# Six column sums of squares as two fp32r products each, with the sums split in place by ScalarE and GpSimd

## The chip, the cores and the metric

The kernel runs on one core of a Trainium2 chip. Times are device microseconds of one launch: the median of three runs was 1108.56 us, from 1108.11 to 1109.01. In the text TensorE is PE, VectorE DVE, ScalarE ACT, GpSimd POOL, and SyncE SP, as in the profile.

## The reference

One residual block on a sequence of 1024 tokens with 1024 features, in float32:

```python
h = rmsnorm(x, g_mix);  z = h @ w_in                      # 1792 columns: LRU input, LRU gate, q, k, v
lx = causal_depthwise_conv(z[..., :512]);  y_lru = rg_lru(lx, ...)
y_lru = rmsnorm(y_lru * gelu(z[..., 512:1024]), g_lru_out)
y_att = rmsnorm(chunk_window_attention(q, k, v, sinks), g_attn_out)
x = x + concatenate([y_lru, y_att]) @ w_out
h = rmsnorm(x, g_ffn);  x = x + square(relu(h @ w_ff1)) @ w_ff2
gate = sigmoid(rmsnorm(x, g_ple) @ w_ple_gate);  x = x + gate * (p @ w_ple_proj)
return rmsnorm(x, g_final)
```

with `rmsnorm(x, g) = x * rsqrt(mean(x * x, axis=-1) + 1e-6) * g`. There are six normalizations, and each needs the sum of squares over the features of every token.

## The kernel before

Activations lie transposed: features on the 128 partitions, tokens along a row. `xT` holds 8 feature tiles of 1024 tokens. Nearly every product is done in three fp32r passes (`passes`, L565 to L569): both operands are split into a high part (fp32r, a rounded copy by ACT) and a low part (the difference, by DVE or POOL), and PE does high by high, high by low and low by high. Halves of 512 tokens are worked one after the other; a PSUM bank holds 128 x 512.

A sum of squares comes about in four steps. ACT squares one feature tile into a ring of two (`square`, L906, or `final_square`). DVE or POOL adds it to a running total of 128 x 512 (`add_square`, L331, or `final_add`, L540), in the tiles `acc` and `acc2`; a square may be written once the one two before it was added (`sq_used`). PE then multiplies the total by a 128 x 128 tile of ones (`sum_rows`, L609), which adds over the partitions and leaves the result on all of them. This product is in plain float32, and the profile shows it as two matmul instructions. ACT takes the root (`root`, L915), DVE inverts it (`invert`, L1286).

There are twelve such sums, two for each of `SS_MIX`, `SS_LRU`, `SS_ATT`, `SS_FFN`, `SS_PLE`, and two of the three parts of `SS_FIN` (512, 256 and 256 tokens; the third part is summed at L874 to L878 and isn't among the twelve). For LRU, PLE and FIN it is POOL that adds the squares.

The order on each engine is the order of the code. Around the six sums of LRU, PLE and FIN it is this:

- LRU. PE runs `group(g)` for g = 0 to 27, each 24 matmuls (5.5 us). Behind group 22 comes the sum of the first half, behind group 23 that of the second, which also waits until ACT has taken the first root (`pe.wait_ge(rms_done, n)`); both use bank 5. Each is followed by a turn of part of v (`turn_v`). Group 24 needs the first half of piece 6 of the weights, split by POOL (`low(12)`, line L444), which stands on POOL right behind the squares' sums. ACT does the squares at g = 20 and 21, reads v at the end of g = 21, and takes the roots at g = 22 and 23.
- PLE. The first sum stands ahead of the gate's cells on PE, the second behind cells 0 to 3. Between the adds of the two, POOL splits four half pieces of the gate's weights.
- FIN. The gate is computed in 20 cells (`CELLS`), each an eight-step product; a cell is 512 tokens wide for q below 12 and 256 for q from 12 on. For each cell DVE scales (`gate_scale`), ACT takes the sigmoid, DVE multiplies and adds into `xT` (`gate_add`), ACT squares, POOL adds. The first sum of FIN stands behind cells 12 and 13 on PE (it covers cells 0 to 3 and 8 to 11, whose last add is q = 11), the second inside cell 17, behind its first step (last add q = 15). The third part is scaled and stored at the end.

Of the kernel before, what the change touches and what calls it, by code (L numbers as in the profile page):

```python
# [13 lines left out]
P = 128  # L14
# [66 lines left out]
RING_FREE = 2  # L81
PRODUCTS = 7
# [11 lines left out]
def build(nc, x, p, vectors, gates_w, w_in, w_out, w_ff1, w_ff2, w_ple_gate, w_ple_proj, alibi, out):  # L94
    ctx = ExitStack()
    with ctx:
# [33 lines left out]
        r_lru = at("r_lru", G + 12 * KB, [P, SEQ])  # L130

# [37 lines left out]
        acc2 = at("acc2", KV + 4 * (PAD + SEQ), [P, SEQ])  # L169

        at_byte = KV + 2 * 4 * (PAD + SEQ)
        small = {}
        for name, shape in (("r_mix", [P, SEQ]), ("ident", [P, P]), ("ones", [P, P]), ("vec", [P, NVEC]),
                            ("nsink", [P, 8]), ("eps", [P, 1]),
                            ("lam", [P, 6, LT]), ("nmax", [P, 2, 8]), ("smax", [P, 2, 8]),
                            ("esink", [P, 2, 8]), ("den", [P, 2, 8])):
            small[name] = at(name, at_byte, shape)
            at_byte += -(-4 * int(np.prod(shape[1:])) // 32) * 32
        r_mix, ident, ones, vec = (small[n] for n in ("r_mix", "ident", "ones", "vec"))
        relu = at("relu", KV + 2 * 4 * (PAD + SEQ), [P, 2, HALF])  # L180
        nsink, eps, lam = (small[n] for n in ("nsink", "eps", "lam"))
# [18 lines left out]

        consts, w_split, sq_used, p_ready, pool_chain = (
# [31 lines left out]
        def half(hf):  # L233
            return slice(hf * HALF, (hf + 1) * HALF)
# [11 lines left out]
        def right(i, h, t):  # L246

            return (h[:, 0:LT, half(1)], t[2], t[1], t[3], h[:, LT:KD, half(0)], h[:, LT:KD, half(1)], t[4])[i]

# [180 lines left out]
        def _(pool):  # L430
# [14 lines left out]

            def sums(n, ring, total):
                for i in range(SQ_TILES[n]):
                    add_square(pool, n, i, ring, total)
# [27 lines left out]
            for n in range(2, IN_PIECES):  # L476
                low(2 * n)
                low(2 * n + 1)
                if n - 2 < LT:
                    gate_input_low(n - 2)  # L480
                if n == 5:
                    sums(SS_LRU, sq, acc)
                    sums(SS_LRU + 1, sq, acc)
# [51 lines left out]
            low(2 * GATE_FIRST + 1)  # L535
            low(2 * (GATE_FIRST + 1))
            low(2 * (GATE_FIRST + 1) + 1)
            sums(SS_PLE + 1, sq2, acc2)

# [13 lines left out]
            for q in range(len(CELLS) - 2):  # L553
                final_add(q)

# [8 lines left out]
        def _(pe):  # L564
# [44 lines left out]
            def sum_rows(n, total, b):  # L609

                pe.wait_ge(sq_used, SQ_BY[n])
                if n >= 1:
                    pe.wait_ge(rms_done, n)
                tok, width = span(n)
                pe.matmul(bank[b][:, 0:width], ones[:, :], total[:, tok], start=True, stop=True  # L615
                          ).then_inc(ss_done, 1)
# [266 lines left out]
        def _(act):  # L883
# [26 lines left out]

            def unit_square(u):
                act.wait_ge(o_read, u + 1)
                square(SQ_BY[SS_ATT - 1] + u, sq, qT[:, 2 * u:2 * u + 2, :, :].rearrange("p c j q -> p (c j q)"))
# [9 lines left out]
            act.activation(lam[:, 2, :], ones[:, 0:LT], ACT.Square)  # L923
            act.wait_ge(first_w_in, 16)
# [49 lines left out]
            for g in range(IN_GROUPS):  # L974
# [16 lines left out]
                if g in (20, 21):  # L991
                    hf = g - 20
                    act.wait_ge(state_done, LT)
                    for j in range(LT):
                        act.wait_ge(y_done, j + 1)
                        square(SQ_BY[SS_LRU + hf] - 4 + j, sq, yl(j)[:, half(hf)])
                if g in (22, 23):
                    root(SS_LRU + g - 22, 5, r_lru, LRU)
# [199 lines left out]
            gate_high(GATE_FIRST)  # L1198
            keep(0)
# [28 lines left out]
            for q in range(len(CELLS)):  # L1228
                if q in (14, 17):
                    root(SS_FIN + (q == 17), 4, r_fin, D)  # L1230
                sigmoid(q)
                if q == 3:
                    root(SS_PLE + 1, 4, r_mix, D)
# [622 lines left out]
```

## Time and profile before

| | us |
| --- | --- |
| median of 3 runs | 1108.56 |
| the profiled execution, its own time | 1109.54 |
| its span | 1107.8 |
| PE busy | 1073.4 (97%) |
| DVE busy | 726.7 (66%) |
| ACT busy | 419.5 (38%) |
| POOL busy | 472.1 (43%) |

The span is the time from the first to the last instruction that the profile shows. Busy times are sums over the whole span; an engine with a low share can still be the one that is waited for in a stretch. The end of a matmul is modelled, so overlapping matmuls are read by their starts: from one start to the next is the time that one really takes of the engine.

### The profile page before, as it was taken

The numbers are of one execution on the slowest core, as the hardware profiler recorded it, in microseconds if no ns is written. First come the engines' busy times: TensorE is split into PE (matmuls) and PEld (weight loads), VectorE is DVE, ScalarE is ACT, GpSimd is POOL, SyncE is SP. The second block draws the span as 40 slices with busy tenths as digits, with TensorE's granted clock in tenths as the row PEclk, the third lists the DMA queues.
The fourth block names the chain that finished last, engine by engine and source line by source line (L and its number), as shares of the span: only waits on it lengthen the run. The fifth ranks groups of instructions, "written<-read, shape, count | busy, mean of one in ns | idle before, by whom it ended". The sixth has DMA issues, their size and how long they took to land.

```text
span 1107.8 us, 13619 instructions
## 1 busy us (share of the span) xinstructions
PE 1073.4 (97%) x4898; PEld 870.7 (79%) x4898; DVE 726.7 (66%) x921; ACT 419.5 (38%) x725; POOL 472.1 (43%) x304
## 2 busy tenths in 40 slices
PE   6899999899999999999999999999999999999995
PEld 5778888677876888888888888888888888888895
DVE  6997666889799836536536546546545545696557
ACT  7555664454456222222222222212312312565334
POOL 2744252333306256255255355355355355293221
PEclk9999999999999999999999999999999999999998
DMA  8211102111001211211211211211111101420004
GB/s 285 77 39 38 38 1 86 39 39 39 1 1 38 76 38 38 76 38 38 76 38 38 76 38 38 76 38 40 73 38 51 63 38 61 167 76 1 1 1 153
DMA packets 20162, 61.05 MB, mean 55 GB/s; under 512 B 2080, under 2 KB 4128, under 8 KB 20128
## 3 DMA queue, kind: packets, MB, share of 16 engines
q1 hardware_dynamic: 19584, 60.08, 15.2%
q10 hardware_dynamic: 544, 0.52, 0.1%
q8 instruction: 20, 0.33, 0.1%
q14 instruction: 14, 0.11, 0.0%
HBM read 56.40 MB, written 4.19 MB: 55 GB/s over the span
## 4 chain that ended last, share of the span: by engine, by line
PE 79%; DVE 11%; ACT 4%; issue 3%; POOL 2%; DMA 1%; SPq 0%; DVEq 0%; ACTq 0%
PE bank L567 26%; PE bank L568 25%; PE bank L569 25%; POOL w_lo L444 1%; DVE r_mix L1288 1%; DVE lane L1335 1%; DMA stage<-in_w_in 1%; DVE acc L343 1%; POOL gx_lo L473 1%; DVE r_ffn L1288 1%; PE bank L657 1%; PE bank L615 1%; DVE xT L1682 1%; DVE h_lo L1550 1%; DVE xT L1754 1%
## 5 line engine op out<-in xcount | busy, mean ns | idle before, releaser
L567 PE MATMUL bank<-h_hi,w_hi 128*128 128x512 f32 (+1 forms) x724 | 282.6, 390 | 13.7 <-DVE h_lo L1275 9.8
L568 PE MATMUL bank<-h_lo,w_hi 128*128 128x512 f32 (+1 forms) x724 | 276.7, 382 | 0.0
L569 PE MATMUL bank<-h_hi,w_lo 128*128 128x512 f32 (+1 forms) x724 | 276.4, 382 | 0.0
L1682 DVE TENSOR_TENSOR xT<-bank,xT 128x512 f32<-128x512 f32 x256 | 173.7, 688 | 114.0 <-PE bank L569 112.3
L567 PE MATMUL bank<-u_hi,w_hi 128*128 128x512 f32 x512 | 202.2, 395 | 2.4 <-DVE xT L1682 1.1
L569 PE MATMUL bank<-u_hi,w_lo 128*128 128x512 f32 x512 | 199.4, 389 | 0.0
L568 PE MATMUL bank<-u_lo,w_hi 128*128 128x512 f32 x512 | 199.4, 389 | 0.0
L567 PEld LDWEIGHTS bank<-h_hi,w_hi 128*128 128x128 f32 x724 | 137.0, 189 | 46.6 <-issue 16.1
L521 POOL TENSOR_TENSOR w_lo<-w_raw,w_hi 128x1024 fp32r<-128x1024 f32 x30 | 78.1, 2624 | 192.2 <-ACT w_hi L1152 192.2
L568 PEld LDWEIGHTS bank<-h_lo,w_hi 128*128 128x128 f32 x724 | 137.0, 189 | 27.0 <-issue 1.9
L569 PEld LDWEIGHTS bank<-h_hi,w_lo 128*128 128x128 f32 x724 | 137.0, 189 | 26.5
L567 PEld LDWEIGHTS bank<-u_hi,w_hi 128*128 128x128 f32 x512 | 96.0, 188 | 32.9 <-issue 7.6
L444 POOL TENSOR_TENSOR w_lo<-stage,w_hi 128x1024 fp32r<-128x1024 f32 x26 | 69.7, 2700 | 114.9 <-ACT w_hi L890 114.9
L569 PEld LDWEIGHTS bank<-u_hi,w_lo 128*128 128x128 f32 x512 | 96.1, 188 | 20.3
L568 PEld LDWEIGHTS bank<-u_lo,w_hi 128*128 128x128 f32 x512 | 96.1, 188 | 19.1
L1146 ACT ACTIVATE relu<-bank 128x512 f32<-128x512 f32 x15 | 9.0, 598 | 193.9 <-PE bank L569 193.9
L505 POOL TENSOR_TENSOR s_raw<-w_raw 128x512 f32<-128x512 f32 x15 | 20.4, 1362 | 144.6 <-DMA w_raw<-in_w_ff 144.6
L514 POOL TENSOR_TENSOR w_lo<-w_raw,w_hi 128x512 fp32r<-128x512 f32 x60 | 78.7, 1324 | 2.3 <-POOL s_raw L510 2.1
L514 POOL TENSOR_TENSOR s_lo<-s_raw,s_hi 128x512 fp32r<-128x512 f32 x45 | 58.9, 1324 | 0.0
L343 POOL TENSOR_TENSOR acc<-acc,sq 128x512 f32<-128x512 f32 x33 | 49.9, 1513 | 17.9 <-DVE acc L343 8.9
L1657 DVE TENSOR_TENSOR usq<-bank,relu 128x512 f32<-128x512 f32 x15 | 10.4, 691 | 68.9 <-PE bank L569 68.9
L1654 DVE TENSOR_TENSOR relu<-bank,relu 128x512 f32<-128x512 f32 x15 | 10.4, 690 | 66.5 <-PE bank L569 66.5
(208 smaller groups left out, 1694.6 us busy)
## 6 DMA issues: line engine op xcount, KB each, us to landing
w_raw<-in_w_ff SPq DMA_DIRECT2D x60, 512.0 KB, 3.7
stage<-in_w_in SPq DMA_DIRECT2D x13, 512.0 KB, 3.4
stage<-in_w_out SPq DMA_DIRECT2D x8, 512.0 KB, 3.5
stage<-in_w_ple_gate SPq DMA_DIRECT2D x8, 512.0 KB, 3.9
xT<-in_x SPq DMA_DIRECT2D x7, 512.0 KB, 9.7
stage<-in_w_ff SPq DMA_DIRECT2D x4, 512.0 KB, 3.2
out_x<-xT SPq DMA_DIRECT2D x4, 512.0 KB, 2.9
out_x<-xT SPq DMA_DIRECT2D x6, 256.0 KB, 2.9
```

The costliest lines, as they stand in the source:

```text
L343: eng.tensor_tensor(dst, dst, src, ALU.add).then_inc(sq_used, 1)
L444: pool.tensor_tensor(lo, stage[:, s % STAGES, :], hi, ALU.subtract).then_inc(w_split, 1)
L473: pool.tensor_tensor(gx_lo[:, half(hf)], yl(j)[:, half(hf)], gx_hi[:, half(hf)], ALU.subtract).then_inc(gx_low, 1)
L505: pool.tensor_tensor(s1, a21, a22, ALU.add).then_inc(s_made, 1)
L514: pool.tensor_tensor(left(i, w_lo, s_lo), left(i, w_raw, s_raw), left(i, w_hi, s_hi), ALU.subtract).then_inc(w1_split, 1)
L521: pool.tensor_tensor(w_lo[:, (FF_FIRST + 1) % 2, o], w_raw[:, (FF_FIRST + 1) % 2, o], w_hi[:, (FF_FIRST + 1) % 2, o], ALU.subtract).then_i ...
L567: pe.matmul(o, whi, hh, start=first, stop=False, skip_group_check=onto)
L568: pe.matmul(o, whi, hl, start=False, stop=False, skip_group_check=onto)
L569: return pe.matmul(o, wlo, hh, start=False, stop=last, skip_group_check=onto)
L615: pe.matmul(bank[b][:, 0:width], ones[:, :], total[:, tok], start=True, stop=True).then_inc(ss_done, 1)
L1288: link(dve.reciprocal(dst[:, span(n)[0]], dst[:, span(n)[0]]))
L1682: dve.tensor_tensor(dst, bank[4 + q % 4][:, :], dst, ALU.add).then_inc(y_added, 1)
```

## The change

Six of the twelve sums, those of LRU, PLE and FIN (`SPLIT_SUMS`), are done as two fp32r products. When all squares of such a sum are added, ACT copies the total into an fp32r tile (`total_head`), and POOL writes total minus that copy, as fp32r, over the total (`total_rest`). PE multiplies both by an fp32r tile of ones, which ACT makes once at the start, into the same bank. PE no longer waits for `sq_used` there but for `total_low`, which POOL raises. The high part lies where the root will be written (`r_lru`, `r_mix`, `r_fin`). The other six sums stay as they are.

```diff
--- before.py
+++ after.py
@@ -79,6 +79,7 @@
 SP_STORES, ACT_STORES = (slice(0, 2), slice(4, 6)), (slice(2, 4), slice(6, 8))
 POOL_OUT, DVE_OUT = (6, 7), range(6)
 RING_FREE = 2
+SPLIT_SUMS = (SS_LRU, SS_LRU + 1, SS_PLE, SS_PLE + 1, SS_FIN, SS_FIN + 1)
 PRODUCTS = 7
 
 
@@ -128,6 +129,8 @@
         lane = at("lane", T + 12 * KB, [P, LT + 1, SEQ])
         gl = at("gl", G, [P, LT, SEQ])
         r_lru = at("r_lru", G + 12 * KB, [P, SEQ])
+        total_lo = at("total_lo", T + 4 * KB, [P, SEQ], F32R)
+        lru_total_hi = at("lru_total_hi", G + 12 * KB, [P, SEQ], F32R)
 
         qT = at("qT", Q, [P, SEQ // CHUNK, LT, CHUNK])
         kT = at("kT", KV, [P, PAD + SEQ])
@@ -167,6 +170,8 @@
         r_fin = at("r_fin", KV, [P, SEQ])
         sq2 = at("sq2", Q + 4 * KB, [P, RING, HALF])
         acc2 = at("acc2", KV + 4 * (PAD + SEQ), [P, SEQ])
+        total2_lo = at("total2_lo", KV + 4 * (PAD + SEQ), [P, SEQ], F32R)
+        fin_total_hi = at("fin_total_hi", KV, [P, SEQ], F32R)
 
         at_byte = KV + 2 * 4 * (PAD + SEQ)
         small = {}
@@ -175,9 +180,13 @@
                             ("lam", [P, 6, LT]), ("nmax", [P, 2, 8]), ("smax", [P, 2, 8]),
                             ("esink", [P, 2, 8]), ("den", [P, 2, 8])):
             small[name] = at(name, at_byte, shape)
+            if name == "r_mix":
+                small["r_mix_r"] = at("r_mix_r", at_byte, shape, F32R)
             at_byte += -(-4 * int(np.prod(shape[1:])) // 32) * 32
         r_mix, ident, ones, vec = (small[n] for n in ("r_mix", "ident", "ones", "vec"))
         relu = at("relu", KV + 2 * 4 * (PAD + SEQ), [P, 2, HALF])
+        ple_total_hi = small["r_mix_r"]
+        ones_r = at("ones_r", at_byte, [P, P], F32R)
         nsink, eps, lam = (small[n] for n in ("nsink", "eps", "lam"))
         nmax, smax, esink, den = (small[n] for n in ("nmax", "smax", "esink", "den"))
         (v_mix, v_conv, v_bconv, v_ba, v_bi, v_lam, v_lru, v_att, v_ffn, v_ple, v_fin, sink) = (
@@ -198,6 +207,7 @@
         out_ready = [sem(f"out_ready{k}") for k in range(KD)]
         out_done = [sem(f"out_done{pair}") for pair in range(KD // 2)]
 
+        total_high, total_low = sem("total_high"), sem("total_low")
         consts, w_split, sq_used, p_ready, pool_chain = (
             sem(n) for n in ("consts", "w_split", "sq_used", "p_ready", "pool_chain"))
 
@@ -246,6 +256,13 @@
         def right(i, h, t):
 
             return (h[:, 0:LT, half(1)], t[2], t[1], t[3], h[:, LT:KD, half(0)], h[:, LT:KD, half(1)], t[4])[i]
+
+        def total_parts(n):
+
+            tok = span(n)[0]
+            if n < SS_PLE:
+                return acc[:, tok], lru_total_hi[:, tok], total_lo[:, tok]
+            return acc2[:, tok], (ple_total_hi if n < SS_FIN else fin_total_hi)[:, tok], total2_lo[:, tok]
 
         def unit_tile(u):
 
@@ -443,6 +460,12 @@
                 lo, hi = w_lo[:, slot(n), o:o + HP], w_hi[:, slot(n), o:o + HP]
                 pool.tensor_tensor(lo, stage[:, s % STAGES, :], hi, ALU.subtract).then_inc(w_split, 1)
 
+            def total_rest(n):
+
+                src, hi, lo = total_parts(n)
+                pool.wait_ge(total_high, 1 + SPLIT_SUMS.index(n) + 1)
+                pool.tensor_tensor(lo, src, hi, ALU.subtract).then_inc(total_low, 1)
+
             def sums(n, ring, total):
                 for i in range(SQ_TILES[n]):
                     add_square(pool, n, i, ring, total)
@@ -479,8 +502,9 @@
                 if n - 2 < LT:
                     gate_input_low(n - 2)
                 if n == 5:
-                    sums(SS_LRU, sq, acc)
-                    sums(SS_LRU + 1, sq, acc)
+                    for n_sum in (SS_LRU, SS_LRU + 1):
+                        sums(n_sum, sq, acc)
+                        total_rest(n_sum)
             low(2 * 7)
             low(2 * 7 + 1)
             probs(0)
@@ -533,9 +557,11 @@
             sums(SS_PLE, sq2, acc2)
             low(2 * GATE_FIRST)
             low(2 * GATE_FIRST + 1)
+            total_rest(SS_PLE)
             low(2 * (GATE_FIRST + 1))
             low(2 * (GATE_FIRST + 1) + 1)
             sums(SS_PLE + 1, sq2, acc2)
+            total_rest(SS_PLE + 1)
 
             def final_add(q):
 
@@ -552,6 +578,8 @@
 
             for q in range(len(CELLS) - 2):
                 final_add(q)
+                if q in (11, 15):
+                    total_rest(SS_FIN + (q == 15))
 
             pool.wait_ge(x_scaled, KD)
             pool.wait_ge(fin_ready, 1)
@@ -608,12 +636,18 @@
 
             def sum_rows(n, total, b):
 
-                pe.wait_ge(sq_used, SQ_BY[n])
                 if n >= 1:
                     pe.wait_ge(rms_done, n)
                 tok, width = span(n)
-                pe.matmul(bank[b][:, 0:width], ones[:, :], total[:, tok], start=True, stop=True
-                          ).then_inc(ss_done, 1)
+                if n in SPLIT_SUMS:
+                    _, hi, lo = total_parts(n)
+                    pe.wait_ge(total_low, SPLIT_SUMS.index(n) + 1)
+                    pe.matmul(bank[b][:, 0:width], ones_r[:, :], hi, start=True, stop=False)
+                    pe.matmul(bank[b][:, 0:width], ones_r[:, :], lo, start=False, stop=True).then_inc(ss_done, 1)
+                else:
+                    pe.wait_ge(sq_used, SQ_BY[n])
+                    pe.matmul(bank[b][:, 0:width], ones[:, :], total[:, tok], start=True, stop=True
+                              ).then_inc(ss_done, 1)
 
             def gates(j):
 
@@ -908,6 +942,12 @@
                     act.wait_ge(sq_used, q - RING + 1)
                 act.activation(ring_tile(ring, q), src, ACT.Square).then_inc(sq_done, 1)
 
+            def total_head(n):
+
+                src, hi, _ = total_parts(n)
+                act.wait_ge(sq_used, SQ_BY[n])
+                act.activation(hi, src, ACT.Copy).then_inc(total_high, 1)
+
             def unit_square(u):
                 act.wait_ge(o_read, u + 1)
                 square(SQ_BY[SS_ATT - 1] + u, sq, qT[:, 2 * u:2 * u + 2, :, :].rearrange("p c j q -> p (c j q)"))
@@ -921,6 +961,7 @@
 
             act.wait_ge(consts, 3)
             act.activation(lam[:, 2, :], ones[:, 0:LT], ACT.Square)
+            act.activation(ones_r[:, :], ones[:, :], ACT.Copy).then_inc(total_high, 1)
             act.wait_ge(first_w_in, 16)
             act.activation(w_hi[:, 0, 0:QP], stage[:, 0, 0:QP], ACT.Copy).then_inc(first_high, 1)
             act.wait_ge(vec_in, 16)
@@ -994,6 +1035,7 @@
                     for j in range(LT):
                         act.wait_ge(y_done, j + 1)
                         square(SQ_BY[SS_LRU + hf] - 4 + j, sq, yl(j)[:, half(hf)])
+                    total_head(SS_LRU + hf)
                 if g in (22, 23):
                     root(SS_LRU + g - 22, 5, r_lru, LRU)
                 if 21 <= g < 25:
@@ -1196,6 +1238,7 @@
             for k in range(KD):
                 ple_high(k, 0)
             gate_high(GATE_FIRST)
+            total_head(SS_PLE)
             keep(0)
             keep(1)
             act.wait_ge(ff2_done, 16 * FF_BLOCKS)
@@ -1229,6 +1272,10 @@
                 if q in (14, 17):
                     root(SS_FIN + (q == 17), 4, r_fin, D)
                 sigmoid(q)
+                if q == 0:
+                    total_head(SS_PLE + 1)
+                if q in (12, 16):
+                    total_head(SS_FIN + (q == 16))
                 if q == 3:
                     root(SS_PLE + 1, 4, r_mix, D)
                 if q in (5, 7):
```

On ACT around the sums of LRU, before (`sq` is the ring of squares, `v_first` and `v_second` are parts of v turned, `r_lru` the root, `w_hi` high parts of weights):

```order
L909 ACTIVATE sq<-lane 128x512 [waits sq_used,y_done,state_done]
L909 ACTIVATE sq<-lane 128x512 [waits sq_used,y_done] x3
L909 ACTIVATE sq<-lane 128x512 [waits sq_used,y_done,state_done]
L909 ACTIVATE sq<-lane 128x512 [waits sq_used,y_done] x3
L1004 ACTIVATE v_first<-bank 128x512 [waits state_done,vt_done]
L919 ACT_TABLE_LOAD
L919 ACTIVATE r_lru<-bank,eps 128x512 [waits ss_done]
L1004 ACTIVATE v_first<-bank 128x512 [waits state_done,vt_done]
L919 ACTIVATE r_lru<-bank,eps 128x512 [waits ss_done]
L1004 ACTIVATE v_second<-bank 128x512 [waits state_done,vt_done]
```

and now (`lru_total_hi` is the high part of the total; L943, L949, L959 and L1046 of the changed kernel are its `square`, `total_head`, `root` and read of v):

```order
L943 ACTIVATE sq<-lane 128x512 [waits sq_used,y_done,state_done]
L943 ACTIVATE sq<-lane 128x512 [waits sq_used,y_done] x3
L949 ACTIVATE lru_total_hi<-acc 128x512 [waits sq_used]
L943 ACTIVATE sq<-lane 128x512 [waits sq_used,y_done,state_done]
L943 ACTIVATE sq<-lane 128x512 [waits sq_used,y_done] x3
L949 ACTIVATE lru_total_hi<-acc 128x512 [waits sq_used]
L1046 ACTIVATE v_first<-bank 128x512 [waits state_done,vt_done]
L959 ACT_TABLE_LOAD
L959 ACTIVATE r_lru<-bank,eps 128x512 [waits ss_done]
L1046 ACTIVATE v_first<-bank 128x512 [waits state_done,vt_done]
L959 ACTIVATE r_lru<-bank,eps 128x512 [waits ss_done]
L1046 ACTIVATE v_second<-bank 128x512 [waits state_done,vt_done]
```

The copy of the second half's total stands ahead of the read of v and of the first root. On POOL at the same place (`acc` is the running total, `w_lo` low parts of weights), before:

```order
L473 TENSOR_TENSOR gx_lo<-lane,gx_hi 128x512 [waits gx_high]
L341 COPY acc<-sq 128x512 [waits sq_used,sq_done,ss_done]
L343 TENSOR_TENSOR acc<-acc,sq 128x512 [waits sq_used,sq_done] x3
L341 COPY acc<-sq 128x512 [waits sq_used,sq_done,ss_done]
L343 TENSOR_TENSOR acc<-acc,sq 128x512 [waits sq_used,sq_done] x3
L444 TENSOR_TENSOR w_lo<-stage,w_hi 128x1024 [waits w_high] x4
L454 TENSOR_TENSOR prob<-prob,den 128x1024 [waits den_done] x2
```

and now:

```order
L496 TENSOR_TENSOR gx_lo<-lane,gx_hi 128x512 [waits gx_high]
L358 COPY acc<-sq 128x512 [waits sq_used,sq_done,ss_done]
L360 TENSOR_TENSOR acc<-acc,sq 128x512 [waits sq_used,sq_done] x3
L467 TENSOR_TENSOR total_lo<-acc,lru_total_hi 128x512 [waits total_high]
L358 COPY acc<-sq 128x512 [waits sq_used,sq_done,ss_done]
L360 TENSOR_TENSOR acc<-acc,sq 128x512 [waits sq_used,sq_done] x3
L467 TENSOR_TENSOR total_lo<-acc,lru_total_hi 128x512 [waits total_high]
L461 TENSOR_TENSOR w_lo<-stage,w_hi 128x1024 [waits w_high] x4
L477 TENSOR_TENSOR prob<-prob,den 128x1024 [waits den_done] x2
```

A subtraction that waits for ACT stands behind each sum, ahead of the next sum's copy and ahead of the weights. On ACT at cells 16 and 17 (`gt` is the gate's tile with the sigmoid, `bank<-xT,vec` is `final_scale`), before:

```order
L1213 ACTIVATE gt<-gt 128x256 [waits gate_scaled] x2
L1220 ACTIVATE sq_105<-xT 128x256 [waits sq_used,x_gated] x2
L1213 ACTIVATE gt<-gt 128x256 [waits gate_scaled]
L1226 ACTIVATE bank<-xT,vec 128x256 [waits sq_done] x2
L919 ACT_TABLE_LOAD
L919 ACTIVATE r_fin<-bank,eps 128x256 [waits ss_done]
L1213 ACT_TABLE_LOAD
L1213 ACTIVATE gt<-gt 128x256 [waits gate_scaled]
L1220 ACTIVATE sq_105<-xT 128x256 [waits sq_used,x_gated] x2
```

and now:

```order
L1256 ACTIVATE gt<-gt 128x256 [waits gate_scaled] x2
L1263 ACTIVATE sq_107<-xT 128x256 [waits sq_used,x_gated] x2
L1256 ACTIVATE gt<-gt 128x256 [waits gate_scaled]
L949 ACTIVATE fin_total_hi<-acc_108 128x256 [waits sq_used]
L1269 ACTIVATE bank<-xT,vec 128x256 [waits sq_done] x2
L959 ACT_TABLE_LOAD
L959 ACTIVATE r_fin<-bank,eps 128x256 [waits ss_done]
L1256 ACT_TABLE_LOAD
L1256 ACTIVATE gt<-gt 128x256 [waits gate_scaled]
L1263 ACTIVATE sq_107<-xT 128x256 [waits sq_used,x_gated] x2
```

The copy of the total stands behind the sigmoid of cell 16.

## Rows read from the trace of the kernel before

**Rows 1.** The page: engine totals, TensorE's group at L567, the costliest squares sum.

```profile
PE 1073.4 (97%) x4898; PEld 870.7 (79%) x4898; DVE 726.7 (66%) x921; ACT 419.5 (38%) x725; POOL 472.1 (43%) x304
...
L567 PE MATMUL bank<-h_hi,w_hi 128*128 128x512 f32 (+1 forms) x724 | 282.6, 390 | 13.7 <-DVE h_lo L1275 9.8
...
L343 POOL TENSOR_TENSOR acc<-acc,sq 128x512 f32<-128x512 f32 x33 | 49.9, 1513 | 17.9 <-DVE acc L343 8.9
```

**Rows 2.** The timeline of TensorE at the LRU sums: start, us, what, [idle before].

```profile
155.07 1.02 PE L615 MATMUL bank<-acc,ones 128*128 128x512 f32 x2
155.93 0.60 PE L641 MATMUL bank<-ident,vT 128*128 128x128 f32 x4
...
157.06 0.40 PE L567 MATMUL bank<-h_hi,w_hi 128*128 128x512 f32 x1
157.30 0.39 PE L568 MATMUL bank<-h_lo,w_hi 128*128 128x512 f32 x1
...
161.85 1.02 PE L615 MATMUL bank<-acc,ones 128*128 128x512 f32 x2
...
163.07 0.47 PE L567 MATMUL bank<-h_hi,w_hi 128*128 128x512 f32 x1
```

**Rows 3.** The timeline of ScalarE there.

```profile
152.40 1.41 ACT L909 ACTIVATE sq<-lane 128x512 f32<-128x512 f32 x2 [0.78 <-POOL acc L343]
154.61 0.63 ACT L909 ACTIVATE sq<-lane 128x512 f32<-128x512 f32 x1 [0.80 <-POOL acc L343]
...
155.74 1.28 ACT L919 ACT_TABLE_LOAD   x1
157.04 0.69 ACT L919 ACTIVATE r_lru<-bank,eps 128x512 f32<-128x512 f32 x1
```

**Rows 4.** The timeline of GpSimd there.

```profile
148.14 4.17 POOL L343 TENSOR_TENSOR acc<-acc,sq 128x512 f32<-128x512 f32 x3
...
153.22 4.15 POOL L343 TENSOR_TENSOR acc<-acc,sq 128x512 f32<-128x512 f32 x3
157.33 4.75 POOL L444 TENSOR_TENSOR w_lo<-stage,w_hi 128x1024 fp32r<-128x1024 f32 x2
```

**Rows 5.** The chain of waits, 140 to 260 us: start, us, what.

```profile
184.21 1.14 PE bank L657 x16
```

**Rows 6.** Timelines of GpSimd, ScalarE and VectorE around the embedding stage.

```profile
980.03 11.29 POOL L444 TENSOR_TENSOR w_lo<-stage,w_hi 128x1024 fp32r<-128x1024 f32 x4
...
992.38 0.63 ACT L909 ACTIVATE sq<-xT 128x512 f32<-128x512 f32 x1 [2.99 <-POOL acc L341]
...
1013.39 0.69 DVE L1734 TENSOR_TENSOR gt<-bank,r_mix 128x512 f32<-128x512 f32 x1 [4.52 <-PE bank L569]
```

**Rows 7.** The timeline of GpSimd at the last two split sums.

```profile
1066.02 3.18 POOL L551 TENSOR_TENSOR acc<-acc,sq 128x512 f32<-128x512 f32 x2 [7.70 <-ACT sq L1220]
...
1079.64 2.01 POOL L551 TENSOR_TENSOR acc<-acc,sq 128x256 f32<-128x256 f32 x2 [6.69 <-ACT sq L1220]
```

**Rows 8.** The timeline of TensorE at the same two sums.

```profile
1070.25 1.02 PE L615 MATMUL bank<-acc,ones 128*128 128x512 f32 x2
...
1081.71 0.70 PE L615 MATMUL bank<-acc,ones 128*128 128x256 f32 x2
```

**Rows 9.** Timelines of ScalarE and VectorE behind the last of them.

```profile
1082.57 0.42 ACT L1213 ACTIVATE gt<-gt 128x256 f32<-128x256 f32 x1 [2.21 <-DVE gt L1734]
...
1086.86 0.42 ACT L1213 ACTIVATE gt<-gt 128x256 f32<-128x256 f32 x1
...
1084.95 0.42 DVE L1734 TENSOR_TENSOR gt<-bank,r_mix 128x256 f32<-128x256 f32 x1 [0.43 <-PE bank L569]
...
1088.60 1.74 DVE L1288 RECIPROCAL r_fin<-r_fin 128x256 f32<-128x256 f32 x1
```

**Rows 10.** TensorE's timeline at 323 us, and a window behind (PEclk is granted clock).

```profile
322.99 0.60 PE L567 MATMUL bank<-h_hi,w_hi 128*128 128x512 f32 x1 [1.83 <-DVE h_lo L1550]
...
324.00:326.00 2.00, 2.00 (x7) 1.54 (x6) 1.97 (x4) 1.26 (x2) 0.00 (x0) 0.50 0.00 0
```

## The prediction

> **What bounds the kernel now.** I read the page first. PE is busy 97% of the span, and one fp32r group of 724 matmuls alone takes 282.6 us [rows 1], so most of the program goes at PE's pace, and a microsecond taken off PE in such a stretch is a microsecond off the end. Then I read PE's timeline at the six sums, with the idle time ahead of each. At five of the six PE comes without a pause and leaves without one; the last waited a little. The chain of waits passes through PE at the sums. So the question is not whether PE's work there counts. It is whether the new operands are there when PE comes. For that I read the timelines of ACT and POOL, which make them.
>
> **What goes away on PE.** A float32 sum of 512 tokens starts at 155.07 and what follows it starts at 155.93: 0.86 us. Two fp32r matmuls start 0.23 us apart (157.06 and 157.30, to a hundredth) [rows 2]. Two products take 0.46 us, so a sum gives back 0.40 us, and the one of 256 tokens half of that. All six give 5 x 0.40 + 0.20 = 2.2 us. That is the most that the change can win.
>
> **What is added.** Each sum gets a copy on ACT and a subtraction on POOL, one behind the other, between the last add and the product. The copy isn't in the trace; its nearest rows are ACT's squares of the same shape, 0.63 us, and the root's 0.69 [rows 3]. The subtraction of 512 is like an add of the same shape: 4.15/3 = 1.38 us with its gap where DVE is quiet [rows 4], 1.51 us on the mean of 33 [rows 1]. An engine sees another's end about 0.1 us later: an add of POOL ends at 148.14 + 4.17 = 152.31 and the waiting square starts at 152.40 [rows 3, 4]. The new delay between last add and product is 0.1 + 0.63 + 0.1 + 1.38 = 2.2 us, and 1.5 us or so for 256 tokens. The copy of the ones runs while the first weights are on their way and costs nothing.
>
> **LRU, first sum.** The adds end at 152.31; copy to 153.05, subtraction to 154.5. PE comes at 155.07 [rows 2], so it doesn't wait, by half a microsecond.
>
> **LRU, second sum.** Here two queues were reordered. On POOL the adds of the second half start 2.15 us later (153.22 becomes 155.35) and end at 159.5. ACT's copy of that total stands ahead of its read of v and of the first root. ACT therefore stands still until 159.6, copies until 160.2, reads v (0.6), loads the root's table (1.28) and takes the first root from 161.9 to 162.6. Before, that root ran at 157.04 [rows 3]. PE's second sum waits for just this root, because both use bank 5. PE would come at 161.85 - 0.40 = 161.45 and waits until 162.7. The sum ends at 163.2, the turn of v (0.36, from the timeline's 163.07 less 162.71) at 163.6. Now group 24 wants POOL's first half of piece 6. POOL started it at 157.33 [rows 4], right behind the adds. It now has two waits and two subtractions ahead: its start goes to 159.5 + 0.1 + 0.63 + 0.1 + 1.38 = 161.75, and with half of 4.75 it ends at 164.1. Group 24 starts at 164.2 instead of 163.07 [rows 2]. So behind both sums PE is 1.15 us later than before, not 0.80 earlier. The second half of the piece ends at 166.5, before its place in the group (167). The scores at 184.21 are PE's own and head the chain that leads through softmax to the next stages [rows 5], so the 1.15 us go to the end. Ends: 0.6 if the two new links take 0.25 less each, 2.0 if DVE's work slows POOL's four new steps to the mean of 1.51 and the weights' subtraction to 2.8 [rows 1, 6].
>
> The Trainium skill, "SBUF — State Buffer", section "SBUF: two separate sides", says that GpSimd and a VectorE operation with two SBUF inputs exclude each other for a whole instruction. The trace's 2.4 us a half piece here against 2.8 at 980 us [rows 4, 6] fits it. By the rule the subtractions behind busy stretches of DVE, the last one above all, would take up to a DVE instruction more, some 0.7 us, which leans to the slow end.
>
> **PLE, two sums.** The subtraction of the first stands behind two halves of weights (980.03 + 11.29/2 = 985.7) and ends at 987.2; PE comes after 990. It delays POOL's next weights and adds by 1.5 us. ACT waited there for POOL's copy until 992.38 [rows 6], so it slips by 1.5 us, and DVE's first scalings with it. At 1013.39 DVE waits 4.52 us for PE [rows 6], which takes this in. PE meets no new wait, and both sums give their 0.40: -0.80.
>
> **FIN, first sum.** POOL's add of q = 11 ends at 1066.02 + 3.18 = 1069.20 [rows 7]. Copy until 1069.93, subtraction (half of 3.18, less the wait within, say 1.45) until 1071.5. PE came at 1070.25 [rows 8] and waits 1.25 us, gains 0.40, and loses 0.1 on restarting: cell 14 is 0.95 late. DVE's scaling of it waits for PE and heads DVE's run of reciprocal and output tiles, so cell 16's sigmoid goes from 1082.57 [rows 9] to 1083.5.
>
> **FIN, second sum.** It is the dearest. The add of q = 15 ended at 1079.64 + 2.01 = 1081.65 [rows 7] and PE took it at once, at 1081.71 [rows 8]. Now ACT makes the copy only behind cell 16's sigmoid: 1083.9 to 1084.3; POOL's subtraction (half of 2.01) ends at 1085.4. PE stands from 1082.7 to 1085.4 in the middle of cell 17. The rest of the cell took from 1081.71 + 0.43 to DVE's scaling at 1084.95 [rows 9], 2.8 us. The scaling moves to 1085.4 + 0.1 + 0.24 + 2.8 = 1088.5. Four more DVE steps of 0.42 follow and the reciprocal of 1088.60 [rows 9] starts at 1090.6. Behind it DVE is the slowest engine to the end, so +2.0 for both FIN sums together. Ends: 1.0, if PE's new slack lets DVE do something else first, and 2.8, by the longer POOL steps.
>
> **The sum.** +1.15 - 0.80 + 2.0 = +2.35 us. The profiled execution took 1109.54 (span 1107.8), so its like would be 1111.9; the median shown is 0.98 lower, and 1108.56 + 2.35 = 1110.9. A difference of 0.2% (2.2 us) is about what can be told from none here, and my number lies just beyond it.
>
> **Rivals.**
> - The clock falls in a stall. At 322.99 PE had stood idle for 1.83 us and the next window shows 0.50, so 1.2 GHz of 2.4 [rows 10]. The new 2.7 us at 1082.7 are longer. At half clock the cell's 2.5 us of matmuls become up to 5; taking two thirds, +1.7: 1112.6. Against it: DVE covers what PE loses behind cell 17. The Trainium skill, "TensorE: Matmul & The Clock Gate", section "What's actually happening", has an idle TensorE fall to 1.2 GHz.
> - Only one place bites. If the copy before the first root or cell 16's sigmoid comes sooner than I think, or the LRU delay is absorbed between 184 and 212 us, where PE has pauses, one term of +1.15 or +2.0 goes: 1109.2.
> - It is faster, which is the other side. The stalls are none if PE really comes later than POOL's new result in all six places; the one that decides is the second LRU sum. If ACT got to the first root before 161.4, and POOL to the weights before 163, the -2.2 would stay: 1106.4. It needs ACT's order to be without effect, and the wait on POOL's adds speaks against it.
> - The change does nothing: fp32r products with ones at 0.43 us each would take the gain, and the stalls be hidden: 1108.6.
>
> **How the numbers follow.** Forecast 0.43, clock 0.23, one place 0.20, nothing 0.06, faster 0.08. The forecast's own range is 1109.8 to 1112.4, from the ends of its terms. For 8 in 10 I go down to 1108.4, into the rival with one place, and up to 1113.4 for the clock. Slower by over 0.2%: the clock's 0.23, six tenths of the forecast (0.26), 0.02 of the rest: 0.51. Faster: 0.09. The same: 0.40.
>
> **What would show it.** At the second LRU sum PE idles some 1.2 us, released by ACT's root, and again half a microsecond at group 24, released by POOL's `w_lo`; the first root runs near 162. At FIN PE idles 1.2 and 2.7 us, released by POOL's low part. The six pairs of products take 0.46 us. At the PLE sums PE doesn't wait. I am wrong if the first root runs before 160, if DVE's last reciprocals are not late against PE's cell 16, or if PE idles at none of the four places.

## The result, and the profile after

The kernel with the split sums took 1115.11 us (median of four runs, 1114.26 to 1115.92), against 1108.62 for the kernel before (four runs, 1108.11 to 1109.01): 6.5 us more, ratio 1.0055 [1.0042, 1.0068]. I had forecast 1110.9 with a range up to 1113.4. The direction was right, the size was not: 6.5 us against 2.35.

The page of the new kernel: engine totals, then PE's group that answers to the one shown before.

```profile
PE 1072.2 (96%) x4898; PEld 870.8 (78%) x4898; DVE 731.4 (66%) x921; ACT 422.9 (38%) x732; POOL 481.7 (43%) x310
...
L595 PE MATMUL bank<-h_hi,w_hi 128*128 128x512 f32 (+1 forms) x724 | 281.6, 389 | 12.4 <-DVE h_lo L1322 8.4
```

Against [rows 1] PE has 1.2 us less to do, ACT 3.4 and POOL 9.6 us more, in seven and six more instructions. DVE has as many instructions as before and 4.7 us more. Nothing in the change gives DVE work, so that number was the first pointer to what I had missed.

**Where the time went.** I compared the starts of the same instructions in both traces. This execution of the new kernel was 0.99 us ahead at PE's sum of 34.75 us (now 33.76), before any of the six split sums runs, so every difference up to FIN has 0.99 added:

| stretch | forecast | measured |
| --- | --- | --- |
| LRU, until group 24 starts | +1.15 | +0.63 |
| LRU, group 24 to the scores | 0 | +2.22 |
| scores to the product at 979.64 (now 981.63) | 0 | +0.13 |
| PLE, until the add of q = 11 | -0.80 | -0.80 |
| FIN, first sum, by the first reciprocal | +0.95 | +0.78 |
| FIN, second sum, by the second reciprocal | +1.05 | +2.91 |
| sum | +2.35 | +5.87 |

The remaining 0.6 us between 5.87 and the medians' 6.5 is within what one execution differs from another here (1114.26 to 1115.92).

PE's timeline at the LRU sums (start, us, what, idle before it), after:

```profile
154.10 0.39 PE L645 MATMUL bank<-lru_total_hi,ones_r 128*128 128x512 f32 x1
154.34 0.39 PE L646 MATMUL bank<-total_lo,ones_r 128*128 128x512 f32 x1
154.57 0.60 PE L675 MATMUL bank<-ident,vT 128*128 128x128 f32 x4
...
161.40 0.50 PE L645 MATMUL bank<-lru_total_hi,ones_r 128*128 128x512 f32 x1 [0.77 <-ACT r_lru L959]
...
161.97 0.60 PE L675 MATMUL bank<-ident,vT 128*128 128x128 f32 x4
162.71 0.47 PE L595 MATMUL bank<-h_hi,w_hi 128*128 128x512 f32 x1
...
179.24 1.16 PE L691 MATMUL bank<-kT,qT 64*128 64x128 f32 x16 [2.16 <-DVE qT L1352]
```

A pair of products takes 0.47 us (154.10 to 154.57) where the float32 sum took 0.86 [rows 2], and the first sum waits for nothing. The second waits for ACT's root. All that was forecast. What was not is the last row: the scores, which stand in the middle of group 26 and wait 2.16 us for DVE. Before, PE came to them without a pause:

```profile
177.38 1.16 PE L657 MATMUL bank<-kT,qT 64*128 64x128 f32 x16
```

ACT's timeline there, after. It answers to [rows 3]: the copy stands ahead of the read of v, the table load and the first root, which runs 4.6 us later than before (160.66 + 0.99 for 157.04).

```profile
158.23 0.63 ACT L949 ACTIVATE lru_total_hi<-acc 128x512 fp32r<-128x512 f32 x1 [2.18 <-POOL acc L360]
...
159.37 1.28 ACT L959 ACT_TABLE_LOAD   x1
160.66 0.69 ACT L959 ACTIVATE r_lru<-bank,eps 128x512 f32<-128x512 f32 x1
```

POOL's timeline there, after, answering to [rows 4]. From the end of the first half's adds (147.15 + 4.16 = 151.31, a row not shown) to the end of its `total_lo` (153.34) it is 2.03 us: this is what the hand-over costs. The four subtractions of weights, of pieces 6 and 7, now run in one row behind the second `total_lo`.

```profile
152.05 1.29 POOL L467 TENSOR_TENSOR total_lo<-acc,lru_total_hi 128x512 fp32r<-128x512 f32 x1 [0.74 <-ACT lru_total_hi L949]
...
158.94 1.30 POOL L467 TENSOR_TENSOR total_lo<-acc,lru_total_hi 128x512 fp32r<-128x512 f32 x1 [0.74 <-ACT lru_total_hi L949]
160.20 9.87 POOL L461 TENSOR_TENSOR w_lo<-stage,w_hi 128x1024 fp32r<-128x1024 f32 x4
```

The timeline of DVE in the kernel before, with POOL's next row beside it, which I had not laid beside these:

```profile
157.76 3.35 DVE L1288 RECIPROCAL r_lru<-r_lru 128x512 f32<-128x512 f32 x1 [1.79 <-ACT r_lru L919]
162.12 0.69 DVE L1305 TENSOR_TENSOR qT<-bank,r_mix 128x512 f32<-128x512 f32 x1 [1.01 <-PE bank L569]
162.73 2.73 DVE L1400 SCALAR_TENSOR_TENSOR lane<-lane,vec,r_lru 128x512 f32<-128x512 f32 x4
165.11 4.97 POOL L444 TENSOR_TENSOR w_lo<-stage,w_hi 128x1024 fp32r<-128x1024 f32 x2 [3.03 <-ACT w_hi L890]
...
174.77 0.69 DVE L1305 TENSOR_TENSOR qT<-bank,r_mix 128x512 f32<-128x512 f32 x1 [2.15 <-PE bank L569]
```

And after:

```profile
161.38 3.35 DVE L1335 RECIPROCAL r_lru<-r_lru 128x512 f32<-128x512 f32 x1 [6.39 <-ACT r_lru L959]
164.77 0.69 DVE L1352 TENSOR_TENSOR qT<-bank,r_mix 128x512 f32<-128x512 f32 x1
165.38 6.57 DVE L1447 SCALAR_TENSOR_TENSOR lane<-lane,vec,r_lru 128x512 f32<-128x512 f32 x4
...
178.50 0.69 DVE L1352 TENSOR_TENSOR qT<-bank,r_mix 128x512 f32<-128x512 f32 x1
```

The four normalizations of the first half of the LRU output (both data inputs in SBUF) took 2.73 us and now take 6.57. The longest took 2878 ns; the median of the eight of both halves is 748. POOL's subtractions beside them took 9.87/4 = 2.47 us each, hardly more than their 4.75/2 = 2.38 before [rows 4]. Before, this DVE work lay in a gap of POOL but for its last 0.35 us: it ran from 162.73 to 165.46, and POOL's piece 6 had ended at 162.08 [rows 4] and piece 7 began at 165.11. The copy of q out of the bank at 178.50 releases the scores. Before, DVE waited for PE ahead of it (1.01 and 2.15 us in the rows above), and the copy was done 1.9 us before PE wanted it: these waits were its reserve. Now DVE works from 161.38 to that copy without a wait. The copy is 4.7 us late (178.50 + 0.99 for 174.77), so the scores are 2.85 us late. The delay of the root alone would have stayed within the reserve, as the run with the pause below shows; the 3.84 us of stretching on top did not.

The chain of waits, after, shows both links (start, us, what):

```profile
160.24 2.33 POOL w_lo L461
162.71 0.47 PE bank L595
...
178.59 0.61 DVE qT L1352
179.24 1.16 PE bank L691 x16
```

**FIN.** PE's timeline, after, beside [rows 8]:

```profile
1072.54 0.47 PE L645 MATMUL bank<-fin_total_hi,ones_r 128*128 128x512 f32 x1 [0.94 <-POOL total_lo L467]
...
1086.56 0.54 PE L645 MATMUL bank<-fin_total_hi,ones_r 128*128 128x256 f32 x1 [2.90 <-POOL total_lo L467]
...
1087.12 0.41 PE L595 MATMUL bank<-h_hi,w_hi 128*128 128x256 f32 x1
1087.33 0.41 PE L596 MATMUL bank<-h_lo,w_hi 128*128 128x256 f32 x1
```

ACT and POOL there (after, [rows 7, 9] before), then DVE:

```profile
1084.54 0.42 ACT L1256 ACTIVATE gt<-gt 128x256 f32<-128x256 f32 x1 [2.22 <-DVE gt L1781]
1084.87 0.40 ACT L949 ACTIVATE fin_total_hi<-acc 128x256 fp32r<-128x256 f32 x1
...
1085.34 1.07 POOL L467 TENSOR_TENSOR total_lo<-acc,fin_total_hi 128x256 fp32r<-128x256 f32 x1 [1.72 <-ACT fin_total_hi L949]
...
1091.09 0.42 DVE L1781 TENSOR_TENSOR gt<-bank,r_mix 128x256 f32<-128x256 f32 x1 [4.13 <-PE bank L597]
...
1093.48 1.75 DVE L1335 RECIPROCAL r_fin<-r_fin 128x256 f32<-128x256 f32 x1
```

The windows (stretch, its length, busy us of PE, PEld, DVE, ACT and POOL, granted clock, DMA share, GB/s):

```profile
1086.00:1088.00 2.00, 1.44 (x7) 1.47 (x8) 0.97 (x1) 1.94 (x4) 0.41 (x1) 0.64 0.87 329
1088.00:1090.00 2.00, 2.00 (x11) 2.00 (x11) 0.00 (x0) 1.13 (x1) 0.00 (x0) 0.50 0.15 51
```

The wait of 2.90 us is the one I had worked out at 2.7, and it came about as I had said: the copy stands behind the sigmoid. Then the granted clock fell to 0.50, so 1.2 GHz. Matmuls start 0.21 us apart instead of 0.12 until 1090.06, and from the sum to DVE's scaling it is 4.53 us, where it had been 3.24 with the float32 sum [rows 8, 9].

### The profile page after: what moved, and what is told of

The parts are those of the page before. It is cut to its first block, busy times and chain, and to the rows that moved or that the text cites. A ratio compares the mean times of both kernels' runs of the same rounds, so it can differ in the third digit from the quotient of the medians.

```text
span 1112.6 us, 13632 instructions
## 1 busy us (share of the span) xinstructions
PE 1072.2 (96%) x4898; PEld 870.8 (78%) x4898; DVE 731.4 (66%) x921; ACT 422.9 (38%) x732; POOL 481.7 (43%) x310
## 4 chain that ended last, share of the span: by engine, by line
PE 75%; DVE 11%; issue 5%; POOL 4%; ACT 4%; DMA 1%; SPq 0%; DVEq 0%; POOLq 0%; ACTq 0%
PE bank L595 25%; PE bank L597 24%; PE bank L596 24%; POOL w_lo L461 1%; DVE r_mix L1335 1%; DVE lane L1382 1%; DVE acc L360 1%; POOL acc L360 1%; POOL gx_lo L496 1%; DMA stage<-in_w_in 1%; PE bank L691 1%; DVE r_ffn L1335 1%; DVE xT L1729 1%; DVE h_lo L1597 1%; ACT prob L1053 1%
```

## The experiments

After its result my theory had two separate causes: at LRU, POOL's run of weight subtractions stretches DVE's normalization; at FIN, the copy's place behind the sigmoid makes a stall that is long enough for the clock to fall. The rivals: that the LRU loss is the late root itself, and that the FIN loss is the stall alone, without the clock.

**One pair of sums at a time.** In the first three kernels only the named sums are split; `total_head` and `total_rest` return at once for the others.

```diff
-SPLIT_SUMS = (SS_LRU, SS_LRU + 1, SS_PLE, SS_PLE + 1, SS_FIN, SS_FIN + 1)
+SPLIT_SUMS = (SS_PLE, SS_PLE + 1)
```

> Only the two sums of PLE are split; LRU and FIN are as before. Theory (the loss lies at LRU and FIN, and PLE gives its whole gain): TensorE doesn't idle before either product pair, the group that follows starts 0.40 us sooner each time, 0.8 us in all, so 1107.8 against 1108.6. Rival (the split costs something everywhere, by the new waits on ScalarE and GpSimd): some 0.5 us slower than before or more.

1107.87 us (1107.42 to 1109.97, 11 runs) against 1108.64, ratio 0.9995 [0.9986, 1.0004]. In its trace the second FIN reciprocal stands 0.80 us nearer to the start of the embedding product than before (108.16 for 108.96). The interval alone couldn't tell this from no change; the trace can.

```diff
+SPLIT_SUMS = (SS_LRU, SS_LRU + 1)
```

> Only the two sums of LRU are split. Theory: GpSimd's weight subtractions now lie beside VectorE's first normalization (4 instructions, 2.7 us before), VectorE takes 6.6 us for it, frees the bank for the scores 2 us late, and TensorE idles 2.2 us ahead of the scores: +2.8 us in all, 1111.4. Rival (only the late first root and the late weights, as in my prediction): +1.2 us, 1109.8, with no idle time of TensorE ahead of the scores.

1112.89 us (1111.61 to 1113.87, 6 runs), ratio 1.0036 [1.0023, 1.0048]: +4.3. The trace has the same picture:

```profile
167.70 6.56 DVE L1451 SCALAR_TENSOR_TENSOR lane<-lane,vec,r_lru 128x512 f32<-128x512 f32 x4
...
181.55 1.16 PE L693 MATMUL bank<-kT,qT 64*128 64x128 f32 x16 [2.17 <-DVE qT L1356]
```

The scores come 3.1 us later against the first turn of v. The profiled execution had also come 0.8 us late to the sum at 34.75 (35.56), so its own span tells little. The median, which other executions make, is about 1 us above what the trace's LRU term says, and I can't place that.

```diff
+SPLIT_SUMS = (SS_FIN, SS_FIN + 1)
```

> Only two sums of FIN are split. Theory: TensorE idles 1 us at the first and 2.9 us at the second, and the granted clock falls behind the second; +3.7 us, 1112.3, and more where the clock falls for longer. Rival (the clock doesn't matter, VectorE covers it): +2.0 to +2.3, 1110.8. With the two others the three parts should add up to the whole: -0.8 + 2.8 + 3.7 = +5.7 of the 6.5 measured.

1112.3 us (1110.91 to 1113.61, 7 runs), ratio 1.0032 [1.0021, 1.0043]: +3.7, and +3.67 by the trace, from the same two places, with a stall of 2.90 us and a fallen clock. So FIN loses as much by itself as together with the others. By the traces' terms the three parts add up to the whole: -0.80 + 3.10 + 3.67 = +5.97, against 5.87. By the medians they give 7.2 against 6.5, a difference that is mostly the unexplained 1 us of the kernel with LRU alone.

**LRU: keep POOL off while DVE normalizes.** Everything else is as in the new kernel.

```diff
+            pool.wait_ge(y_normed, LT)
             low(2 * 7)
             low(2 * 7 + 1)
```

> The changed kernel, but GpSimd waits ahead of piece 7 of the weights until VectorE has normalized the first half of LRU's output (4 instructions). Nothing else is moved. Theory (the two engines get in each other's way in SBUF): the 4 instructions take 2.7 us again instead of 6.6, VectorE frees the bank in time, TensorE doesn't idle ahead of the scores, and the whole is 1.5 to 2.2 us faster than the changed kernel: 1113.2. Rival (the 6.6 us come from elsewhere): they stay, and the time stays at 1115 or gets worse, since piece 7 is later.

1112.49 us (1112.07 to 1113.64, 5 runs), ratio 1.0036 [1.0023, 1.005]: 2.6 us less than the changed kernel. Its timelines of DVE, POOL and PE:

```profile
165.69 2.73 DVE L1448 SCALAR_TENSOR_TENSOR lane<-lane,vec,r_lru 128x512 f32<-128x512 f32 x4
...
168.50 4.76 POOL L461 TENSOR_TENSOR w_lo<-stage,w_hi 128x1024 fp32r<-128x1024 f32 x2 [3.26 <-DVE lane L1448]
...
177.30 1.16 PE L692 MATMUL bank<-kT,qT 64*128 64x128 f32 x16
```

The root is as late as in the changed kernel (160.97), DVE's four steps are back at 2.73 and PE has no pause at the scores. From the turn of v ahead of the first sum (148.49) to the scores it is 28.81 us, against 28.21 before (from 149.17) and 31.05 after (from 148.19). The collision is worth 2.2 us by the trace (2.6 by the medians). The late root and the late weights alone leave +0.60, which is what they cost less the 0.8 us that the products save.

**LRU: root ahead of the copy.** This takes one of the two delays from the root and leaves POOL's order.

```diff
-                    total_head(SS_LRU + hf)
+                    if hf == 0:
+                        total_head(SS_LRU)
                 if g in (22, 23):
                     root(SS_LRU + g - 22, 5, r_lru, LRU)
+                if g == 22:
+                    total_head(SS_LRU + 1)
```

> The changed kernel, but ScalarE copies the total of the second LRU half behind the first LRU root instead of ahead of it. Theory: the first root runs near 156.5 us as before, VectorE's reciprocal and first normalization start 4 us sooner; the normalization then overlaps GpSimd's adds rather than the weights. TensorE's wait at the second sum is set by the copy and subtraction (about 0.3 us), and it doesn't idle ahead of the scores: 2 us faster than the changed kernel, 1113.1. Rival (GpSimd's later queue alone is what matters, not ScalarE's order): it stays at 1115.

1114.24 us (1113.91 to 1114.97, 5 runs), ratio 1.005 [1.0037, 1.0064]: only 0.9 less than the changed kernel. Its timelines of POOL, DVE and PE:

```profile
160.77 10.80 POOL L461 TENSOR_TENSOR w_lo<-stage,w_hi 128x1024 fp32r<-128x1024 f32 x4
...
162.96 9.16 DVE L1450 SCALAR_TENSOR_TENSOR lane<-lane,vec,r_lru 128x512 f32<-128x512 f32 x4
...
163.28 0.47 PE L595 MATMUL bank<-h_hi,w_hi 128*128 128x512 f32 x1 [1.19 <-POOL w_lo L461]
```

I had expected more: that the root would be back near 156.5 and that an earlier normalization would lie beside POOL's adds. The root ran at 158.24, which is 2.8 us sooner than in the changed kernel on one clock and still 1.8 us later than before, since the squares ahead of it wait for POOL's adds. And the normalization met more of the weights, not less. Three of the four steps fell beside subtractions of weights, 9.16 us in all (three times some 2.15 more than before), and PE waited 1.19 us for the weights instead of 0.77 for the root. The scores still wait 1.75 us for DVE, and from the turn of v to the scores it is 30.90 us for 31.05. So a root that comes 2.8 us earlier gains 0.15 us by the trace while POOL's run stands where it is. With the pause, which left the root late and gained 2.2 us, this speaks against the rival with the late root. No run here has the root quite at its old time with POOL's new order.

**FIN: the copy ahead of the sigmoid of cell 16.**

```diff
+                if q == 16:
+                    total_head(SS_FIN + 1)
                 sigmoid(q)
...
-                if q in (12, 16):
-                    total_head(SS_FIN + (q == 16))
+                if q == 12:
+                    total_head(SS_FIN)
```

> The changed kernel, but ScalarE copies the total of the second FIN sum ahead of cell 16's sigmoid instead of behind it. Theory (the stall of 2.9 us is the wait for that sigmoid, and it makes the clock fall): the copy comes 1.8 us sooner, TensorE idles about 1 us instead of 2.9, the clock stays at full, and the time falls by 1.8 + 1.4 = 3.2 us: 1111.9. Rival (VectorE alone sets this stretch): the stall shrinks, but the time falls by under 1 us.

1111.55 us (1110.81 to 1113.35, 8 runs), ratio 1.0027 [1.0016, 1.0038]: 3.6 less than the changed kernel.

```profile
1085.23 0.36 PE L645 MATMUL bank<-fin_total_hi,ones_r 128*128 128x256 f32 x1 [1.36 <-POOL total_lo L467]
```

The stall shrinks to 1.36 us, the granted clock stays at 1.00 from 1080 to 1100, and both FIN sums together cost 0.64 us by the trace instead of 3.7. Stall and clock go together here, so this run doesn't part them. The next does.

**FIN: the same wait, but PE is kept busy in it.** Twenty further matmuls write the bank that the sum then overwrites.

```diff
+                    if n == SS_FIN + 1:
+                        for _ in range(20):
+                            pe.matmul(bank[b][:, 0:width], w_hi[:, 1, 0:P], h_hi[:, 0, tok], start=True, stop=True)
                     pe.wait_ge(total_low, SPLIT_SUMS.index(n) + 1)
```

> The changed kernel with 20 fp32r matmuls of 256 tokens added on TensorE ahead of its wait at the second FIN sum (2.4 us of work in a stall of 2.9 us; their result is overwritten). Theory (the clock falls because TensorE stands idle): the granted clock stays at full in 1086 to 1090 us, the rest of cell 17 takes 2.8 us instead of 4.3, and the time falls by 1.4 us: 1113.7. Rival (the clock is without effect on the end, or it falls for another reason): no change, or slower by what the added work overruns.

1113.79 us (1112.29 to 1114.3, 5 runs), ratio 1.0042 [1.0028, 1.0056]: 1.3 less than the changed kernel, although PE does more. PE's timeline, and the window behind:

```profile
1083.41 2.56 PE L646 MATMUL bank<-h_hi,w_hi 128*128 128x256 f32 x20
1086.38 0.39 PE L648 MATMUL bank<-fin_total_hi,ones_r 128*128 128x256 f32 x1 [0.41 <-POOL total_lo L467]
...
1086.00:1088.00 2.00, 1.62 (x13) 1.62 (x14) 0.88 (x1) 1.97 (x3) 0.33 (x1) 1.00 0.87 330
```

The sum starts no earlier, but the clock stays at 2.4 GHz and DVE's scaling comes 3.06 us behind the sum instead of 4.53. The clock's share is 1.5 us, and what is left of FIN is +2.12 by the trace. This is my forecast of +2.0, without the clock. The share differs a little between executions: in the traces of the pause and of the earlier root, with the same stall and the same fall, DVE's scaling comes 4.16 and 4.26 us behind the sum.

**Both cures in one kernel** (the pause on POOL and the early copy, all six sums split):

> The changed kernel with both mends: GpSimd waits with piece 7 until VectorE has normalized the first half, and ScalarE copies the second FIN total ahead of cell 16's sigmoid. Theory (two separate causes): the gains of 2.6 and 3.5 us add up, 1115.1 - 6.1 = 1109.0, level with the kernel before. Rival (both mends free the same wait, or the second gain came from a run with a luckier clock): 1110.5 or more.

1109.09 us (1108.57 to 1109.88, 11 runs) against 1108.55, ratio 1.0004 [0.9995, 1.0013]. The gains of the two edits add up (2.6 + 3.6 = 6.2 by their own medians, 6.0 measured), so the causes are separate, and together they are 6.0 of the 6.5 us. Six split sums are then worth nothing: what the products save, the stalls of 1.34 us and 0.94 us at FIN and the late second LRU sum take.

**Two attempts at a gain.** The first leaves FIN as it was and splits LRU and PLE, with the root ahead of the copy, the pause, and the first half of piece 6 ahead of the adds, so that group 24 finds it:

```diff
...
                 if n == 5:
+                    low(2 * 6)
...
+            pool.wait_ge(y_normed, LT)
             low(2 * 7)
...
```

> The sums of PLE and LRU are split, FIN is not. At LRU, ScalarE copies the second total behind the first root, GpSimd splits the first half of piece 6 ahead of the squares' adds and waits with piece 7 until the first normalization is done. Theory: no instruction of VectorE with two SBUF inputs meets GpSimd's weights for long, and the copy no longer holds up the root, so TensorE idles at most 0.4 us at either LRU sum: -0.8 at PLE, -0.8 + 0.5 at LRU, 1107.5. Rival (the two more steps of GpSimd can't be hidden at LRU in any order): 1108.5 or more, above the kernel that splits PLE alone (1107.9).

1109.06 us (1108.51 to 1111.39, 11 runs), ratio 1.0007 [0.9998, 1.0016]: no gain. Its timelines of POOL, DVE and PE:

```profile
144.06 2.42 POOL L461 TENSOR_TENSOR w_lo<-stage,w_hi 128x1024 fp32r<-128x1024 f32 x1 [16.25 <-ACT w_hi L929]
...
144.43 4.67 DVE L1451 TENSOR_TENSOR lane<-lane,gl 128x1024 f32<-128x1024 f32 x2
...
155.29 0.47 PE L650 MATMUL bank<-lru_total_hi,ones_r 128*128 128x512 f32 x1 [0.80 <-POOL total_lo L469]
```

The moved subtraction fell beside another DVE operation with two SBUF inputs, which took 4.67 us (2.35 for the same two before), and the squares, the adds and the first sum came late behind it. It is the same collision in another place. From the turn of v to the scores it is 29.28 us for 28.21; how much of this +1.07 is the collision and how much the second sum's wait of 0.62 us for `total_lo` no run parts.

The second splits only the sums with slack, both of PLE and the first of LRU, and keeps the pause:

```diff
+SPLIT_SUMS = (SS_LRU, SS_PLE, SS_PLE + 1)
...
+            pool.wait_ge(y_normed, LT)
             low(2 * 7)
```

> The sums of PLE and the first of LRU are split, with GpSimd's wait ahead of piece 7. Theory: ScalarE's copy of the first total delays the adds of the second by 2.2 us; they end ahead of TensorE's sum by 2 us still, piece 6 ends just ahead of its group, and the first root is late by 2 us; gain 0.8 + 0.4: 1107.4. Rival (VectorE's later reciprocal and normalization meet GpSimd's piece 6): 1108.2 or more.

1107.43 us (1107.05 to 1108.37, 11 runs) against 1108.55 (27 runs), ratio 0.9989 [0.998, 0.9998]: 1.1 us faster than before, as the three pairs' 3 x 0.40 say. The interval only just leaves out no change; the trace has the same gain, 27.81 us from the turn of v to the scores for 28.21 and 0.80 at PLE. PE's timeline at LRU:

```profile
154.06 0.39 PE L648 MATMUL bank<-lru_total_hi,ones_r 128*128 128x512 f32 x1
...
160.43 1.02 PE L652 MATMUL bank<-acc,ones 128*128 128x512 f32 x2
...
175.96 1.16 PE L694 MATMUL bank<-kT,qT 64*128 64x128 f32 x16
```

PE has no pause at either sum or at the scores. It is the fastest version of this case, by a tenth of a per cent.

## Why the prediction was right in direction and too small

- **PE's saving: right.** 0.39 to 0.40 us a pair of 512; -0.80 at PLE in the changed kernel and in the one with PLE alone.
- **LRU, ACT and POOL in a row: right in mechanism.** First root forecast at 161.9, found at 160.66 + 0.99 = 161.65; the sum forecast at 162.7, found at 162.39; group 24 at 164.2, found at 163.70, released by POOL's weights as the chain says. The term until there was +1.15 and is +0.63, since each of the two hand-overs took 2.0 us and not 2.2, and POOL had had 0.16 us to spare between the two halves' adds.
- **LRU, "the scores at 184.21 are PE's own": the step that failed.** I followed PE, ACT and POOL and took DVE to be in time. It had 2.15 us to spare at 174.77, and more ahead of it. The delayed root moved its normalization by 3.64 us (165.38 + 0.99 for 162.73), beside POOL's undivided run, and there it took 3.84 us more. The Trainium skill, "SBUF — State Buffer", section "SBUF: two separate sides", has the rule that a VectorE operation with two SBUF inputs and a GpSimd one exclude each other. The trace agrees, and the prediction used it only to lengthen POOL's steps. Here DVE lost most: up to 2.88 us for a step of 0.74, while POOL's took 2.47 on the mean. The pause on POOL took this term away (31.05 to 28.81 us), and the kernel with the earlier root made it larger in DVE's row (9.16 us).
- **FIN, first sum: right.** Wait 0.94 (forecast 1.25), +0.78 (forecast +0.95).
- **FIN, second sum: the stall was right, 2.90 for 2.7, the term was not.** The sum left out the clock, which I had given as a rival with +1.7; its price was 1.5 us. I had argued against it that DVE covers what PE loses. DVE waited 4.13 us for PE at just that place, so it covered nothing.
- **What the two are worth.** The traces' +5.87 lies 3.5 us above the forecast's +2.35. DVE's term at LRU, put at nothing, is 2.2 of them and the clock 1.5; the other terms nearly cancel.
- **The range.** Added up straight, the terms' own ends give 1109.4 to 1112.6 and not the 1109.8 to 1112.4 that stand there. The measured 1115.11 is outside of both and above the wider range's 1113.4, too.
- **The rivals.** The clock was true but as an addition to the forecast, not instead of it; "only one place bites" fell, as both bit; "faster" fell for the reason that I gave.

## What to carry to other kernels

Work that is taken from the bounding engine and handed to two idle ones pays only where its input is ready earlier than the hand-over takes, here 2.0 us; check that for each place, not for the change as a whole: three of six had the slack and gave 1.1 us, the other three lost some 7 by the traces (5.87 + 1.2). When a step moves in time, lay the timelines of all engines beside its new place, those too that the change doesn't touch, and ask which of their operations share SBUF with it. A new stall of the matmul engine can be priced twice, as idle time and as the slower matmuls behind it; the second price falls due only where another engine waits for those matmuls.

## What the runs showed of the hardware

- A GpSimd run of 128x1024 subtractions without a gap stretched VectorE's 128x512 operations with two SBUF inputs from 0.74 us to as much as 2.90, about one subtraction each, and was itself lengthened less (2.47 us each beside 2.38 in the changed kernel, and 2.70 in the one with the earlier root, where three of DVE's steps lay beside it). VectorE's copies out of a bank (0.69 us) and its reciprocal (3.35 us) kept their times beside the same run.
- The same at FIN, smaller: in the changed kernel DVE's add into `xT` at 1071.45, with two SBUF inputs, took 1.22 us instead of 0.42 beside the subtraction of the first total (1071.12, 1.27 us). DVE waits 2.68 us for PE two steps later, so it cost nothing.
- A stall of 2.89 or 2.90 us at the second FIN sum was followed by a granted clock of 0.50 in all four traces that have it, for 3.5 us in the changed kernel; stalls of 1.36 and 1.34 us there were not. Stalls of 1.76 to 1.83 us between 321 and 328 us were followed by a fall in three traces (the kernel before [rows 10] among them) and by none in nine others, so at that length the trace of before alone couldn't say. Twenty further matmuls in the stall of 2.9 us kept the clock.
- The falls near 323 cost nothing in the end: from the first scores to the first product of the embedding it is 802.26, 802.43 and 802.43 us in the three traces with one and 802.25 to 802.52 in the nine without. At FIN, where DVE waits for PE, a fall cost 1.5 us.
- Why the kernel with LRU alone is about 1 us slower in its median than its trace explains stays open.
